# Final norm turned to tokens on partitions, and the norms' spreads taken from the root column, in a two-layer diffusion backbone

## The reference

```python
def rms_norm(x, g):
    xf = x.astype(jnp.float32)
    y = xf * lax.rsqrt(jnp.mean(xf * xf, axis=-1, keepdims=True) + EPS)
    return (y * g.astype(jnp.float32)).astype(x.dtype)

hx = modulate(rms_norm(x, g_mix[l]), sh1, sc1)                    # ahead of the mixer
x = x + gt2 * conv_ffn(modulate(rms_norm(x, g_ffn[l]), sh2, sc2), ...)
return rms_norm(x, g_final)                                       # [1, 256, 1024]
```

## Time and profile before

| | us |
|---|---|
| median of 3 runs | 1298.58 |
| lowest and highest | 1296.21, 1299.73 |
| the profiled execution | 1299.9 |
| its span, first to last instruction | 1298.1 |
| TensorE busy | 1261.2 (97% of the span) |
| VectorE busy | 883.4 (68%) |
| ScalarE busy | 552.4 (43%) |
| GpSimd busy | 293.3 (23%) |

### The profile page before, as it was taken

The page is one execution under the profiler, slowest core; times in us unless marked ns, Lnnn a source line. Parts: engine busy times, 40 slices in busy tenths (PEclk is TensorE's granted clock), DMA queues, the critical chain, the costliest instruction groups (busy, mean ns, idle before and its releaser), DMA issues.

```text
span 1298.1 us, 19916 instructions
## 1 busy us (share of the span) xinstructions
PE 1261.2 (97%) x7670; PEld 1091.1 (84%) x7670; DVE 883.4 (68%) x1205; ACT 552.4 (43%) x872; POOL 293.3 (23%) x247
## 2 busy tenths in 40 slices
PE   5999999999999999999999999999999998999997
PEld 3688777777788798888888888998889998999997
DVE  4596788753699677663779674586786656755654
ACT  4222355654333245332223332343676545743543
POOL 0005299210042101111001110002792220220220
PEclk9999999999999999999999999999999998999999
DMA  9365511212356335563555663334433544664561
GB/s 374 147 222 166 175 61 61 74 62 70 118 183 235 129 99 166 192 194 117 174 158 187 207 213 122 104 123 153 143 119 119 184 156 133 204 212 146 178 211 34
DMA packets 50339, 198.76 MB, mean 153 GB/s; under 512 B 5584, under 2 KB 6992, under 8 KB 49104
## 3 DMA queue, kind: packets, MB, share of 16 engines
q1 hardware_dynamic: 50256, 197.62, 46.4%
HBM read 196.55 MB, written 1.05 MB: 152 GB/s over the span
## 4 chain that ended last, share of the span: by engine, by line
PE 88%; DVE 7%; ACT 2%; issue 1%; DMA 1%; SPq 0%; DVEq 0%; ACTq 0%
PE psA L523 25%; PE psA L525 24%; PE psA L524 24%; PE psB L523 2%; PE psB L525 2%; PE psB L524 2%; DVE w_lo L1261 2%; PE psB L778 1%; PE psA L762 1%; PE psB L790 1%; ACT w_hi L947 1%; DVE acc L1537 1%; PE psB L705 1%; PE psB L544 1%; DVE small L1550 1%
## 5 line engine op out<-in xcount | busy, mean ns | idle before, releaser
L523 PE MATMUL psA<-h_hi,w_hi 128*128 128x256 f32 (+1 forms) x1528 | 521.5, 341 | 5.4 <-DVE h_lo L1414 2.6
L525 PE MATMUL psA<-h_hi,w_lo 128*128 128x256 f32 (+1 forms) x1528 | 514.1, 336 | 0.0
L524 PE MATMUL psA<-h_lo,w_hi 128*128 128x256 f32 (+1 forms) x1528 | 514.0, 336 | 0.0
L947 ACT ACTIVATE w_hi<-raw 128x1024 fp32r<-128x1024 f32 (+2 forms) x244 | 276.9, 1138 | 285.6 <-PE psA L525 214.1
L1261 DVE TENSOR_TENSOR w_lo<-raw,w_hi 128x1024 fp32r<-128x1024 f32 (+2 forms) x244 | 336.1, 1378 | 89.4 <-ACT w_hi L947 89.4
L523 PEld LDWEIGHTS psA<-h_hi,w_hi 128*128 128x128 f32 x1528 | 291.6, 191 | 40.1 <-issue 7.7
L525 PEld LDWEIGHTS psA<-h_hi,w_lo 128*128 128x128 f32 x1528 | 291.6, 191 | 29.7
L524 PEld LDWEIGHTS psA<-h_lo,w_hi 128*128 128x128 f32 x1528 | 291.9, 191 | 28.6 <-issue 0.2
L512 POOL TENSOR_TENSOR hid_lo<-sig,hid_hi 128x512 f32 (+3 forms) x44 | 67.3, 1529 | 474.9 <-ACT hid_hi L1226 474.9
L1282 DVE SCALAR_TENSOR_TENSOR ada_sum<-raw,csil,ada_sum 128x1024 f32<-128x1024 f32 x112 | 154.6, 1412 | 0.0
L523 PE MATMUL psA<-hid_hi,w_hi 128*128 128x256 f32 (+1 forms) x352 | 116.4, 331 | 2.2 <-DVE sig L1732 2.1
(11 more groups left out here) (194 smaller groups left out, 1488.4 us busy)
## 6 DMA issues: line engine op xcount, KB each, us to landing
raw<-w_up SPq DMA_DIRECT2D x88, 512.0 KB, 4.3
raw<-w_ada SPq DMA_DIRECT2D x80, 512.0 KB, 3.7
raw<-w_dn SPq DMA_DIRECT2D x32, 704.0 KB, 5.3
raw<-w_in SPq DMA_DIRECT2D x36, 512.0 KB, 4.3
raw<-w_at SPq DMA_DIRECT2D x24, 512.0 KB, 3.5
raw<-w_fn SPq DMA_DIRECT2D x16, 640.0 KB, 4.4
raw<-w_sc SPq DMA_DIRECT2D x16, 640.0 KB, 3.9
raw<-w_cf SPq DMA_DIRECT2D x16, 640.0 KB, 3.9
```

The source lines that it names most:

```text
L523: pe.matmul(out, w0, hi, start=first, stop=False)
L524: pe.matmul(out, w0, lo, start=False, stop=False)
L525: return pe.matmul(out, w1, hi, start=False, stop=last)
L947: act.activation(w_hi[:, s, 0:tiles * P], raw[:, r, 0:tiles * P], ACT.Copy).then_inc(head_done, 1)
```

## The change

Three edits. First, in all norms the spread is made from the column itself: the stationary operand is a column of root_col repeated 128 times, the moving one the identity. The identities scaled by VectorE (two per stream, four at the start) and the semaphore inv_col ahead of them are gone. Second, the last norm: GpSimd multiplies blocks 0 to 6 of X by their gain into x_g as soon as each is written, and VectorE does block 7. TensorE turns each 128x128 piece of x_g, so that tokens stand on partitions; four pieces fill a bank, four banks hold the result. There is no spread here: the inverse root is one number per partition, and VectorE (tokens 0 to 127) and ScalarE (128 to 255) multiply it in as they read the banks. The order on TensorE is: first half of the mean, four transposes of tokens 0 to 127, second half of the mean, the four of tokens 128 to 255, then blocks 4 to 7 of both. Third, the output is [2, 128, 1024] and goes out in four transfers of 256 KB, in rows of 2 KB, each when its bank has been read. The host no longer turns it.

```diff
-        y_out = at("y_out", [KD, SEQ], F32, h_off)
+        x_g = at("x_g", [KD, SEQ], F32, h_off)
+        y_out = at("y_out", [2, D], F32, h_off + 4 * KD * NT)
+        row_bank = [psB[1], psB[2], psB[3], psA[0]]
 # SyncE
-            for kk in range(KD):
-                sp.wait_ge(fin, kk + 1)
-                sp.dma_start(io["out"][:, kk, :], y_out[:, kk, :]).then_inc(stored, 16)
-            sp.wait_ge(stored, 16 * KD)
+            for piece in range(4):
+                side, t = divmod(piece, 2)
+                sp.wait_ge((fin, fin_act)[t], side + 1)
+                sp.dma_start(io["out"][t, :, 512 * side:512 * side + 512], y_out[:, t, 512 * side:512 * side + 512])\
+                    .then_inc(stored, 16)
+            sp.wait_ge(stored, 16 * 4)
 # GpSimd
+            for kk in range(KD - 1):
+                pool.wait_ge(evac, PER_LAYER + START["dn1"] + kk + 1)
+                pool.tensor_scalar(x_g[:, kk, :], X[:, kk, 0:SEQ], V("g_final", kk), 0.0, ALU.mult, ALU.add)\
+                    .then_inc(x_scaled, 1)
 # TensorE, spread_inverse; the same at the start
-                    mm = pe.matmul(spread_bank[s][:, b * P:(b + 1) * P], M("mean"), sqb[:, b * P:(b + 1) * P],
-                                   start=True, stop=True)
+                    mm = pe.matmul(spread_bank[s][:, b * P:(b + 1) * P], root_col[:, b:b + 1].to_broadcast([P, P]),
+                                   M("ident"), start=True, stop=True)
-            norm_stat(2 * DEPTH)
+            def final_mean(squares, last):
+                for b in range(2):
+                    mm = pe.matmul(psB[0][:, b:b + 1], squares[:, b * P:(b + 1) * P], M("mean")[:, 0:1],
+                                   start=(not last and b == 0), stop=last, skip_group_check=True)
+                if last:
+                    mm.then_inc(stat, 1)
+            def turn_rows(kk, t):
+                if kk < KD - 1:
+                    pe.wait_ge(x_scaled, kk + 1)
+                else:
+                    pe.wait_ge(x_scaled_last, 1)
+                mm = pe.transpose(row_bank[2 * (kk // 4) + t][:, (kk % 4) * P:(kk % 4 + 1) * P],
+                                  x_g[:, kk, t * P:(t + 1) * P], M("ident"))
+                if kk % 4 == 3:
+                    mm.then_inc(rows, 1)
+            pe.wait_ge(evac, PER_LAYER + START["dn1"] + 1)
+            pe.wait_ge(sq_sum, SUMMED[2 * DEPTH] + 6)
+            final_mean(sqa, False)
+            for kk in range(4):
+                turn_rows(kk, 0)
+            pe.wait_ge(sq_last, normed(2 * DEPTH, 0) - 2)
+            final_mean(sqb, True)
+            for kk in range(4):
+                turn_rows(kk, 1)
+            for t in range(2):
+                for kk in range(4, KD):
+                    turn_rows(kk, t)
 # ScalarE
+            act.wait_ge(inv, normed(2 * DEPTH, 0))
+            for side in range(2):
+                act.wait_ge(rows, 2 * side + 2)
+                act.activation(y_out[:, 1, 512 * side:512 * side + 512], row_bank[2 * side + 1][:, :], ACT.Copy,
+                               scale=root_col[:, 1:2]).then_inc(fin_act, 1)
 # VectorE, inverse_root; the same at the start
-                dve.reciprocal(root_col[:, 2 * s:2 * s + 2], root_col[:, 2 * s:2 * s + 2]).then_inc(inv_col, 1)
-                dve.wait_ge(inv_col, normed(r, s))
-                for b in range(2 * s, 2 * s + 2):
-                    op = dve.tensor_scalar(sqb[:, b * P:(b + 1) * P], M("ident"), root_col[:, b:b + 1], float(D),
-                                           ALU.mult, ALU.mult)
-                op.then_inc(inv, 1)
+                dve.reciprocal(root_col[:, 2 * s:2 * s + 2], root_col[:, 2 * s:2 * s + 2]).then_inc(inv, 1)
 # VectorE, the end
+            dve.wait_ge(evac, TOTAL)
+            dve.tensor_scalar(x_g[:, KD - 1, :], X[:, KD - 1, 0:SEQ], V("g_final", KD - 1), None, ALU.mult)\
+                .then_inc(x_scaled_last, 1)
             inverse_root(2 * DEPTH, 0)
-            dve.wait_ge(spread, normed(2 * DEPTH, 0))
-            for kk in range(KD):
-                dve.scalar_tensor_tensor(y_out[:, kk, :], X[:, kk, 0:SEQ], V("g_final", kk), spread_bank[0][:, 0:SEQ],
-                                         ALU.mult, ALU.mult).then_inc(fin, 1)
+            dve.wait_ge(inv, normed(2 * DEPTH, 0))
+            for side in range(2):
+                dve.wait_ge(rows, 2 * side + 1)
+                dve.tensor_scalar(y_out[:, 0, 512 * side:512 * side + 512], row_bank[2 * side][:, :],
+                                  root_col[:, 0:1], None, ALU.mult).then_inc(fin, 1)
```

More of the change, by code:

```diff
@@ L287, in program @@
         ada_acc, reduced = sem("ada_acc"), sem("ada_reduced")
-        folded, v_mm, v_done, inv_col, spread, sq_last, half_done, x_half = map(sem, (
-            "folded", "v_mm", "v_done", "inv_col", "spread", "sq_last", "half_done", "x_half"))
+        folded, v_mm, v_done, spread, sq_last, half_done, x_half = map(sem, (
+            "folded", "v_mm", "v_done", "spread", "sq_last", "half_done", "x_half"))
         tap_pool = sem("tap_pool")
@@ L303, in program @@
         cv, silu, hid_head, hid_rest, fin = map(sem, ("cv", "silu", "hid_head", "hid_rest", "fin"))
+        fin_act, x_scaled, x_scaled_last, rows = map(sem, ("fin_act", "x_scaled", "x_scaled_last", "rows"))
         def M(name, n=128, off=0):
@@ L658, in _ @@
             for b in range(4):
-                mm = pe.matmul(spread_bank[b // 2][:, b * P:(b + 1) * P], M("mean"), sqb[:, b * P:(b + 1) * P],
-                               start=True, stop=True)
+                mm = pe.matmul(spread_bank[b // 2][:, b * P:(b + 1) * P], root_col[:, b:b + 1].to_broadcast([P, P]),
+                               M("ident"), start=True, stop=True)
             mm.then_inc(spread, 2)
@@ L1429, in _ @@
             dve.wait_ge(root, 2)
-            dve.reciprocal(root_col[:, :], root_col[:, :]).then_inc(inv_col, 2)
-            dve.wait_ge(inv_col, 2)
-            for b in range(4):
-                op = dve.tensor_scalar(sqb[:, b * P:(b + 1) * P], M("ident"), root_col[:, b:b + 1], float(D),
-                                       ALU.mult, ALU.mult)
-            op.then_inc(inv, 2)
+            dve.reciprocal(root_col[:, :], root_col[:, :]).then_inc(inv, 2)
             for ahead in range(2):
@@ L1865 @@
     io = {name: nc.dram_tensor(name, x.shape, F32, kind="ExternalInput").ap() for name, x in arrays.items()}
-    io["out"] = nc.dram_tensor("out", (P, KD, SEQ), F32, kind="ExternalOutput").ap()
+    io["out"] = nc.dram_tensor("out", (SEQ // P, P, D), F32, kind="ExternalOutput").ap()
     program(nc, io)
     r = run(nc, [arrays], core_ids=[0])
-    return np.ascontiguousarray(r.results[0]["out"].transpose(2, 1, 0).reshape(1, SEQ, D))
+    return np.ascontiguousarray(r.results[0]["out"].reshape(1, SEQ, D))
```

## The result

The changed kernel takes 1291.63 us (median of 7 runs, 1290.77 to 1292.25), the kernel before 1297.74 in the same comparison (7 runs, 1295.58 to 1299.73). By these medians it is faster by 6.1 us, a ratio of 0.9953; the ratio on record is 0.9947, 95% interval 0.9938 to 0.9957, and 0.9947 is the new median over 1298.58, the old one of three runs.

A forecast was written before the change was run, and what follows sets the result against it. TensorE was taken to be busy 97% of the span, so only its waits could gain. Tail 2.15, layer 1's norms 0.52 and 0.40, and front 0.8 sum to 3.9 us: 1298.58 to 1294.7, range 1292.3 to 1297.0.

The forecast's parts named there:

- The last norm's chain: Waits from the last product to the first output issue: that issue would start 1.06 us sooner, 2.9 to 3.0 after the last matmul.
- -2.37 for -2.15: Whole tail from last matmul to end: predicted -2.15 us, bounds -1.85 to -2.5, by shorter chain and four larger transfers.
- Layer 1's norm between mixer and MLP: Bare one-stream norm: identities and their handover go, spread costs the same, -0.52 us.
- Layer 1's first norm: Second stream's identities leave VectorE's chain, shortening the rotation wait: -0.40 us, or 0 if the loop catches on a matmul.
- Layer 0's norm: Norm between mixer and MLP of layer 0: both streams lie inside matmuls, so 0 gain.
- the front's "-0.8": First norm at the start: four identities leave the chain, so the spread starts sooner; -0.8 us taken.
- bound of -0.45: First norm: if the clock comes up at the same moment as before, half the saving is lost, -0.45 us.
- bound of -0.91: First norm: if all the rest moves with the earlier spread, the full saving of -0.91 us.
- run-to-run switching point: TensorE's clock gate: the skill says switching varies by run, which would turn part of the clock rivals into scatter; no size.
- The clock at the layer 1 norm stays up: Norm between mixer and MLP: shorter pause may keep TensorE's clock up, 2.2 us more, total -6.1, 1292.5 us; chance 0.17.
- Only the bare ends gain: Savings at the front and layer 1's first norm don't come through; 2.7 us remain, 1295.6 with half the front; chance 0.18.
- The way out becomes the bound: Output transfers: four large stores run slowly; at 157 GB/s the gain is eaten, at 95 GB/s 1302.9 us; chance 0.04.

The follow-up runs named there:

- f_old: Front of the kernel alone (both layers, last norm and way out left out) with the old norm: 66.6 to 70.4 us, mean 68.23 together with its repeat.
- f_old2: Repeat of f_old, the front alone with the old norm, for more executions: mean of both together 68.23 +- 0.46 us.
- e8_eight_out: Changed kernel with each of its four output transfers cut in two (128 KB, 1 KB rows): 1295.09 us, ratio 0.9974 against the kernel before.
- f_new: f_old with the first norm's spread made from the column: 66.4 to 66.9 us, mean 67.05 +- 0.32 together with its repeat.
- e4_slow_start: Changed kernel with four unread scaled identities put back on VectorE ahead of the first spread: 1294.65 us, ratio 0.9986 against the kernel before.
- e1_col_all: Kernel before with only the first edit, in all norms, and the old last norm and output: 1294.93 us, ratio 0.9985 against the kernel before.
- e2_col_start: Kernel before with the first edit at the first norm only: 1295.95 us, ratio 0.9995 against the kernel before.
- e5_after_again: Changed kernel run again without any edit, beside the kernel before: 1293.33 us, ratio 0.9962.
- e6_before_again: Kernel before run again without any edit, for a second profile: 1298.67 us, ratio 1.0001 against the kernel before.
- g_after: Whole changed kernel run once more without any edit, beside the kernel before: 1292.96 us, ratio 0.9965.

## Why the prediction was wrong

**The steps that held.** The last norm's chain: first issue 2.96 behind the residual's start, where 2.92 follows from the prediction's own times; reads of a bank 0.71 and 0.69 for 0.69; four transposes 0.63 for 0.60; nothing held up by transposes or block 7. Issues 0.48 apart. First byte 0.87 behind the first issue; 1.05 MB in 2.8 us, as chosen between 2.5 and 3.1; only some 0.2 was not foreseen (0.9 from the last byte to the end, for 1.1). -2.37 for -2.15. Layer 1's norm between mixer and MLP: -0.52 for -0.52, the spread 1.24 for 1.23, so the repeated column costs nothing. Layer 1's first norm: -0.5 for -0.40, and -0.5 in the table's last column, four kernels against six. Layer 0's norm: 0. For the front only the direct part held, 0.65 to 0.91. The sum of what the steps really have, with 0.65 to 0.91 in the front, is 4.0 to 4.3 for 3.87.

**The step that failed** is the front's "-0.8". Its bound of -0.45 held TensorE's clock to the moment at which it came up before, and its bound of -0.91 let that moment move with the work; neither let it come up 6 us sooner. The difference of the profiled executions is -3.2 there. That moment is not a property of the kernel: it lies at 30 us or at 36 to 37 in executions of the same front (f_old and f_old2; after and e8_eight_out), and the one is worth 2.5 to 3 us over the other. The profile that the prediction was built on happened to have a late one. Beside it the sum had no term at all for layer 0's attention, where the two profiles differ by 1.8, another draw. For the front, the term that should have stood in the sum is the mean over the draws, -1.2 +- 0.6 as f_old and f_new measure it, and its range should have been some 3 us wide, not 0.5. The prediction named the run-to-run switching point and left it without a width: it counted "about 1 us" for medians, while single executions of the kernel before have a standard deviation of 1.1 to 1.8 in the five comparisons.

**The base.** The prediction subtracted from 1298.58, the median of three; seven runs gave 1297.74. From there its sum gives 1293.9, and the miss of size is 2.2; the whole range would have been 1291.5 to 1296.2, with the result just inside. So that the result fell out of the range is due as much to the base as to the front.

**How much is real.** The three comparisons give -6.1, -5.0 and -4.5 us, each with an error of 0.6 to 0.9; weighted together -5.4 +- 0.4. The steps have some 4.2. So of the first result's 6.1 some 0.7 is its own draw, and 1.2 +- 0.4 stay over the steps. A shift in the draws of the front (0.3 to 0.5 +- 0.6 over the direct gain) may hold a part of it, and the mean of e4_slow_start points the same way, those of e1_col_all and e2_col_start the other. The draw in the attention hardly holds it: it was long more often with the whole change. The rest stays open.

**The rivals.** "The clock at the layer 1 norm stays up", -6.1, has the right number and is wrong. In the changed kernel the granted clock is down there, and where it is still up at the spread it falls a little later, as in e5_after_again:

```profile
1086.00:1088.00 2.00, 0.71 (x4) 0.52 (x4) 1.01 (x3) 0.41 (x2) 0.00 (x0) 0.90 0.43 168
1088.00:1090.00 2.00, 1.16 (x5) 1.19 (x6) 1.75 (x5) 1.09 (x3) 0.00 (x0) 0.50 0.00 0
...
1094.00:1096.00 2.00, 2.00 (x17) 2.00 (x17) 1.35 (x3) 1.27 (x2) 0.00 (x0) 0.89 0.00 0
```

Its spread took 0.72 instead of 1.24, and the products behind it ran at the slow pace for longer. From the mean at that norm to the first issue of the output it is 201.9 there and 201.6 in the profile after; in the kernel before 203.4 with the late fall (e6_before_again) and 203.1 with the early one. Where the clock falls moves 0.3 in these pairs; that it falls was the same in all of them. The changed kernel's third profile, g_after, has 202.2, so this stretch too has a draw, of some 0.6. What staying up would bring was not seen in any run. "Only the bare ends gain" is refuted by the 403.7 of layer 1 and by e1_col_all. "The way out becomes the bound" came true in form only: the bytes, at 380 GB/s, are now what ends last there, far above the 157 GB/s at which the gain would have been eaten.

## What to carry to other kernels

Look at two executions of the kernel before you price an edit near a pause: a clock that comes up late in the one profile at hand may be a draw, as it was here, and then has to enter the sum as a mean and the range at its full width. Output that left through one queue in pieces of 128 KB was paced by its issues, 0.48 us each; with pieces twice as large the bytes were the bound. A factor that is one number per partition needs no spread at all once the result is turned. Turning cost nothing here: the first four transposes ran while TensorE waited for the square, and the last were through at 1285.26, before the queue came to their bank (its fourth issue ends at 1287.00).

## What the runs showed of the hardware

- In these traces the granted clock reads 1.00 from the start of an execution to its first fall, also where the durations (634 ns for 385) show the lower level.
- A matmul whose stationary operand is one column of SBUF repeated 128 times costs what a plain one does: 1.24 us for 1.23, and 2.08 for 2.08 at the start.
- Stores in rows of 2 KB moved 389 GB/s in a window with a recorded share of 1.06, those in rows of 1 KB 358 in one with the same share:

```profile
1296.60:1296.80 0.20, 0.00 (x0) 0.00 (x0) 0.00 (x0) 0.00 (x0) 0.00 (x0) 0.50 1.06 358
```

The Trainium skill (DMA: Bandwidth & Descriptors, "Where 436 GB/s comes from") has HBM transfers bound at about 358 for one core's share. With one core at work the stores of 2 KB rows lie above it here, at 380 over their whole stretch, as did the loads with 421.
- GpSimd's scaling of a block takes 0.48 us alone and 2.04 where it starts 0.18 behind a VectorE operation with two operands in SBUF, which a second such operation follows:

```profile
1262.29 0.48 POOL L523 TENSOR_SCALAR x_g<-X,vec 128x256 f32<-128x256 f32 x1 [10.77 <-DVE X L1726]
1265.30 2.04 POOL L523 TENSOR_SCALAR x_g<-X,vec 128x256 f32<-128x256 f32 x1 [2.53 <-DVE X L1726]
```

```profile
1265.12 1.61 DVE L1305 TENSOR_TENSOR w_lo<-raw,w_hi 128x1408 fp32r<-128x1408 f32 x1
1266.65 0.42 DVE L1381 TENSOR_TENSOR sqa<-sqa,sqb 128x256 f32<-128x256 f32 x1
```

Three of the seven scalings were so held, all well ahead of need. The prediction had given each 0.76 from a block of the same width read with a stride.
